# Dot products, key rounds and key products in another order, an inverse's steps cut into quarters, in a fused RWKV-7 and convolution block

## The chip, the cores and the metric

The kernel runs on one core of one Trainium2 chip. The metric is the device time in microseconds of one execution, the median of three runs. TensorE is called PE here, VectorE DVE, ScalarE ACT, GpSimd POOL, and SyncE, which only issues DMAs in this kernel, SP.

## The reference

One layer of a model of width 2048 over 256 tokens, batch 1, in float32. A vector `c` modulates it (shift, scale, gate, twice), then come an RWKV-7 mixer, a feed-forward with a causal convolution of 3 taps and hidden width 5504, and after them a second block. Cut to what matters here:

```python
mod = silu(c) @ ada_w + ada_b            # six vectors of 2048 = 12288 dot products
h = rms(x) * (1 + scale1) + shift1
r, k, v = x_rkv @ w_rkv                  # three 2048x2048 projections
w = decay(w0 + tanh(xw @ w1) @ w2); a = sigmoid(a0 + (xa @ a1) @ a2)
kk = k * k_k; kk = kk * rsqrt(sum(kk*kk, per head))   # "key rounds"
state = state*w + (state a) b + v k      # 256 steps, 32 heads of 64
x = x + gate1 * rms((y * g) @ w_o)
h = rms(x) * (1 + scale2) + shift2
u = conv3(h @ w_in); f = (silu(gate) * val) @ w_out
x = x + gate2 * rms(f)                   # then the second block
```

## The kernel before

Everything lies transposed in SBUF: 16 tiles of 128 channels by 256 tokens. The recurrence is worked in 4 chunks of 64 tokens, with the inverse of a triangular 64x64 matrix for each head and chunk.

**The ring.** Nearly all weights come through `ring`, four slots of 1 MB, which SP fills in a fixed order. The load at position p of that order waits until position p-4 has been used. A load holds one output tile of a projection (`wv`, `wr`, `wo`, `fi`, `fo`) or 128 rows of `ada_w`.

**The dots.** `ada_w` is transposed on the host, so that an output of `mod` is a dot product of one partition's row with `cb` (silu(c) in every partition). One instruction on DVE, line 1683, makes 128 of them from a slot of 1 MB, in place. There are 96: 0 to 31 before the first normalisation, 32 to 37 (two slots of `zb`, loads by POOL, line 565) before the work that prepares keys and decays, 38 to 61 in the ring between tiles of v's projection (two loads of `ada_w` ahead of each load of `wv` from the fifth on), 62 to 79 in the ring during the four chunks of the scan (4, 6, 6, 2), and 80 to 95 in the 16 tiles of the output projection wo, one each, with loads by POOL (line 605). DVE counts them in `ada_used`.

**The keys.** After the dots DVE has a fixed list: elementwise work and prefix sums (1844, 1851), then eight rounds b of the key norm (1869 to 1871), and after rounds 1, 3, 5 and 7 `scaled_keys(q)` (1859 to 1863), which needs rounds 2q and 2q+1 and two exponentials that ACT makes into buffers `px`, `tmp` or `zb` (1354, 1355). The Gram products on PE (844) wait for the fourth `scaled_keys`.

**v and the inverse.** PE projects v in 16 tiles (line 679, 16 matmuls each, evacuated by ACT, 1391). After tiles 8 to 12 it runs one step of the inverse each: two transpositions of the inner inverse (874), one more (884), and two products (893, 902). A step is 64 to 256 small matmuls into four banks of PSUM, and ACT evacuates a bank at a time (1397 to 1410). The scan then alternates between PE (934, 984, 995), DVE (1935 and others) and ACT.

**Split projections.** wo and everything after it works at higher precision: ACT makes `whi` from half a weight slot (1231), DVE subtracts it to get `wlo` (1705), and PE does two matmuls per 128 rows (702, 703), 32 a tile. ACT copies the result out (1238), DVE adds the low part (1713, `join`). For the feed-forward's input `fi` DVE also does two convolution taps per tile (2040, 2041), the first on ACT (1497). `y_lo_part`, line 1974, makes the low part of wo's other operand, and wo's second half waits for the last of them.

**Norms.** The squares of wo's and fo's tiles are summed as the tiles come, by POOL (589, 622); then PE sums over the partitions (661). A third norm, of the sum with the residual (1753, 1755), has its squares on ACT (1200) and is summed on PE (666). The residual is spilled to HBM by a DMA that ACT issues (1475).

PE's order in v, and behind it the line that makes the order of SP's loads there:

```python
for k in range(NT):
    project("v", mixb, k)
    if k == 8:
        pe.wait_ge(base_rdy, 1)
        turned(0)
    elif k == 9:
        turned(1)
```

```python
for _k in range(NT):
    RV += [("v", _k)] + [("ada", len(RV) - NT - _k + _j) for _j in range(0 if _k < 4 else 2)]
```

Of the kernel before, what the change touches and what calls it, by code (L numbers as in the profile page):

```python
# [36 lines left out]
S = 256  # L37
# [22 lines left out]
          ("w2", 1, NT, NT, 0), ("a2", 1, NT, NT, 0), ("r", NT, NT, NT, 0), ("v", NT, NT, NT, 0), ("ada", 42, 0, 0, 0),  # L60
# [24 lines left out]
assert len(RV) == 74 and len(RV_UNIT) == 74  # L85
# [88 lines left out]
def build(nc, t, out, stage=99, dbg=None):  # L174
    with ExitStack() as ctx:
# [87 lines left out]
        ld_ada = [[sem(f"ld_ada{q}_{j}") for j in range(6 - 4 * q)] for q in range(2)]  # L263
# [40 lines left out]
        ld_adw = [sem(f"ld_adw{j}") for j in range(4)]  # L304
        rexp = sem("rexp")
# [114 lines left out]

        MIX = {"r": 0, "k": 1, "v": 2, "w": 3, "a": 4, "g": 5}
        MIX_BUF = {"r": mixa, "v": mixb}
        ADA_PARTS = [(0, 32, 6), (32, 38, 2)]
        ADA_REST = 38
        ada_w = lambda j: ada2[:, j, :] if j < 2 else flat_h[:, 2048 * (j - 2):2048 * (j - 1)]

        def ada_slot(part, j):

            return ada2[:, j, :] if part else ada4[:, j, :] if j < 4 else ada2[:, j - 4, :]
# [127 lines left out]
        def _(pool):  # L557
            def ada(part):
                lo, hi, n = ADA_PARTS[part]

                def load(j, it):

                    src = t["ada"][lo + j] if it is None else \
                        t["ada"][bass.ds(it * n + lo + j, 1)].rearrange("o p n -> (o p) n")
                    pool.dma_start(ada_slot(part, j), src).then_inc(ld_ada[part][j], 16)

                for j in range(n):
                    load(j, None)
                with pool.Fori(1, (hi - lo) // n) as it:
                    for j in range(n):  # L570
                        pool.wait_ge(ada_used, it * n + (lo + j + 1 - n))
                        load(j, it)

            pool.wait_ge(ada_used, 32)
            ada(1)
# [9 lines left out]
            def wo_square(i):  # L585
                pool.wait_ge(tile_free, TILE["wo"] + i + 1)
                if i:
# [7 lines left out]
            for j in range(NT):  # L595
# [7 lines left out]
                if j >= 4:  # L603
                    pool.wait_ge(ada_used, 80 + j - 3)
                pool.dma_start(ada_w(j % 4), t["ada"][80 + j]).then_inc(ld_adw[j % 4], 16)
# [4 lines left out]

            pool.wait_ge(x_spill, 16)
            pool.wait_ge(pe_step, STEP["fo"])
# [37 lines left out]
        def _(pe):  # L651
# [3 lines left out]
            def rms(k, sq, summed=0):  # L655
# [7 lines left out]
                for i in range(NT):  # L663
                    if i % 4 == 0:
                        pe.wait_ge(rms_sq[k], i // 4 + 1)
# [1648 lines left out]
```

## Time and profile before

| | |
|---|---|
| median of 3 runs | 2020.38 us (2018.16 to 2024.25) |
| the profiled execution's own time | 2022.18 us |
| its span, first to last instruction | 2020.5 us |
| granted clock of PE, mean | 0.988 |
| PE busy | 1950.3 us, 97% |
| DVE busy | 1437.4 us, 71% |
| ACT busy | 907.3 us, 45% |
| POOL busy | 107.7 us, 5% |
| moved by DMA | 418.31 MB, mean 207 GB/s |

Busy time is that of instructions; "idle before" names what an engine was released by. A weight load on PE (PEld) overlaps the matmul before it. With PE at 97% the sum of its waits is some 70 us, and what an edit is worth shows in those waits.

### The profile page before, as it was taken

What the parts mean: (1) busy time and instruction counts of PE and PEld (TensorE: products, weight loads), DVE (VectorE), ACT (ScalarE), POOL (GpSimd) and SP (SyncE); (2) the same over time, 40 slices, a digit from 0 to 9 for tenths busy, and PEclk for the clock granted to TensorE, in tenths of its full rate; (3) what the DMA queues carried; (4) which work ended last, traced back from release to release, by engine and by line L of the source; (5) the groups of instructions that cost most, each with busy time, mean ns of one, the idle gap of its engine ahead of it and who ended that gap; (6) DMA issues with size and microseconds to landing.
All of it is one profiled execution on the core that took longest, in us unless ns stands there. A gap on an engine that the chain in (4) does not pass through costs nothing.

```text
span 2020.5 us, 33348 instructions
## 1 busy us (share of the span) xinstructions
PE 1950.3 (97%) x12886; PEld 1688.3 (84%) x12886; DVE 1437.4 (71%) x2023; ACT 907.3 (45%) x1474; POOL 107.7 (5%) x111
## 2 busy tenths in 40 slices
PE   6999899898898989999999999999999999999998
PEld 4888788797887878888888888888878888888887
DVE  7996959535858977777777776444467967766876
ACT  4346221042334545555555555444455436545554
POOL 0000002000002300000000000000010000002200
PEclk9999999899999999999999999999999999999999
DMA  9996414667637925555555556555535544446553
GB/s 393 421 374 213 146 68 162 274 249 298 239 132 285 383 101 187 187 187 187 187 185 186 181 190 230 179 193 193 193 123 213 186 167 175 159 146 222 180 184 124
DMA packets 58933, 418.31 MB, mean 207 GB/s; under 512 B 6673, under 2 KB 7057, under 8 KB 12561
## 3 DMA queue, kind: packets, MB, share of 16 engines
q1 hardware_dynamic: 54514, 383.36, 51.4%
q0 software_dynamic: 3888, 27.26, 3.4%
q10 hardware_dynamic: 432, 6.29, 0.8%
q8 instruction: 70, 1.15, 0.2%
q14 instruction: 29, 0.24, 0.0%
HBM read 410.60 MB, written 6.29 MB: 206 GB/s over the span
## 4 chain that ended last, share of the span: by engine, by line
PE 85%; DVE 8%; DMA 3%; issue 2%; ACT 1%; POOL 1%; SPq 0%; DVEq 0%; POOLq 0%; ACTq 0%
PE ps L702 42%; PE ps L703 21%; PE ps L679 9%; PE ps L803 3%; DVE ring L1683 2%; DMA ring<-in_wv 1%; PE ps L798 1%; DVE ar L1870 1%; DMA bk<-in_ada 1%; PE ps L819 1%; DVE mixb L1921 1%; PE ps L1074 1%; POOL h L601 1%; PE ps L1149 0%; PE ps L768 0%
## 5 line engine op out<-in xcount | busy, mean ns | idle before, releaser
L702 PE MATMUL ps<-x_pair,whi 128*128 128x512 f32 x2464 | 879.1, 401 | 5.3 <-issue 2.8
L703 PE MATMUL ps<-x_pair,wlo 128*128 128x256 f32 x2464 | 692.7, 281 | 0.0
L1705 DVE TENSOR_TENSOR wlo<-ring,whi 128x1024 fp32r<-128x1024 f32 x468 | 547.5, 1206 | 104.7 <-ACT whi L1231 97.2
L702 PEld LDWEIGHTS ps<-x_pair,whi 128*128 128x128 f32 x2464 | 464.3, 188 | 125.1 <-issue 12.0
L1231 ACT ACTIVATE whi<-ring 128x1024 fp32r<-128x1024 f32 x468 | 462.3, 1031 | 96.5 <-PE ps L703 93.8
L703 PEld LDWEIGHTS ps<-x_pair,wlo 128*128 128x128 f32 x2464 | 466.7, 189 | 0.3
L1238 ACT ACTIVATE px<-ps 128x256 f32<-128x256 f32 x202 | 77.8, 385 | 463.3 <-PE ps L703 463.3
L702 PE MATMUL ps<-hid_pair,whi 128*128 128x512 f32 x688 | 238.8, 391 | 0.0
L703 PE MATMUL ps<-hid_pair,wlo 128*128 128x256 f32 x688 | 192.7, 280 | 0.0
L679 PE MATMUL ps<-mixb,ring 128*128 128x256 f32 x640 | 147.5, 393 | 9.0 <-DMA ring<-in_wv 9.0
L702 PEld LDWEIGHTS ps<-hid_pair,whi 128*128 128x128 f32 x688 | 128.7, 187 | 28.5 <-DVE wlo L1705 0.3
L1683 DVE CUSTOM_DVE_ANT_0 ring<-ring,cb,prm 128x2048 f32<-128x2048 f32 x42 | 97.5, 2347 | 74.1 <-DMA ring<-in_ada 73.4
L679 PEld LDWEIGHTS ps<-mixb,ring 128*128 128x128 f32 x640 | 125.8, 198 | 28.7 <-DMA ring<-in_wv 10.2
L703 PEld LDWEIGHTS ps<-hid_pair,wlo 128*128 128x128 f32 x688 | 130.0, 189 | 0.0
L679 PE MATMUL ps<-mixa,ring 128*128 128x256 f32 x512 | 113.2, 384 | 0.0
L679 PEld LDWEIGHTS ps<-mixa,ring 128*128 128x128 f32 x512 | 98.2, 192 | 13.8
L1713 DVE TENSOR_TENSOR px<-ps,px 128x256 f32<-128x256 f32 x134 | 56.4, 421 | 68.4 <-ACT px L1238 68.3
L2040 DVE SCALAR_TENSOR_TENSOR tmp<-px,prm,tmp 128x255 f32<-128x255 f32 x86 | 41.6, 484 | 83.7 <-ACT tmp L1497 83.7
L1768 DVE TENSOR_TENSOR px<-ps,px 128x256 f32<-128x256 f32 x68 | 28.8, 424 | 95.4 <-ACT px L1238 95.1
L702 PE MATMUL ps<-y_pair,whi 128*128 128x512 f32 x256 | 90.4, 397 | 5.2 <-DVE y_pair L1974 3.6
L803 PE MATMUL ps<-mixb,ring 128*128 128x256 f32 x384 | 86.6, 382 | 0.0
L1497 ACT ACTIVATE tmp<-px,prm 128x256 f32<-128x256 f32 x86 | 51.8, 602 | 74.7 <-DVE px L1713 74.7
(297 smaller groups left out, 2308.3 us busy)
## 6 DMA issues: line engine op xcount, KB each, us to landing
ring<-in_fi SPq DMA_DIRECT2D x86, 1024.0 KB, 4.8
ring<-in_zin SPq DMA_DIRECT2D x52, 1024.0 KB, 4.8
ring<-in_ada SPq DMA_DIRECT2D x42, 1024.0 KB, 6.6
ring<-in_fo SPq DMA_DIRECT2D x32, 1024.0 KB, 4.8
bk<-in_ada SPq DMA_DIRECT2D x22, 1024.0 KB, 16.3
ring<-in_wr SPq DMA_DIRECT2D x16, 1024.0 KB, 4.8
ring<-in_wv SPq DMA_DIRECT2D x16, 1024.0 KB, 8.9
ring<-in_wo SPq DMA_DIRECT2D x16, 1024.0 KB, 7.0
```

The costliest lines, as they stand in the source:

```text
L679: last = mm(ps[0:m, bank, 0:S], w[:, k * m:(k + 1) * m], act[:, k, :], start=k == 0, stop=k == n - 1)
L702: mm(ps[:, bank, 0:2 * S], w_h, pair_k, start=first and k == 0, stop=False)
L703: m = mm(ps[:, bank, 0:S], w_l, pair_k[:, 0, :], start=False, stop=last and k == n - 1)
L803: last = mm(outer_bank(m), ring[:, i % RING, m * P:(m + 1) * P], mixb[:, i, :], start=i == 0 and m % 2 == 0, stop=i == NT - 1, skip_group_ ...
L1231: A(whi[:, hf % WB, 0:m], ring[:, u % RING, 1024 * x:1024 * x + m], ACT.Copy).then_inc(w_hi, 1)
L1238: A(part[:, (TILE[name] + k) % 4, :], ps[:, (TILE[name] + k) % BANKS, S:2 * S], ACT.Copy).then_inc(x_part, 1)
L1497: A(tmp[:, (k % 4) * S:(k % 4 + 1) * S], join_in("fi", k, it), ACT.Identity, scale=param_at("fcw", 4 * FT, kk), bias=param_at("fcb", 0, kk ...
L1683: V.tensor_tensor_reduce(out=w, in0=w, in1=cb[:], scale=1.0, scalar=prm[:, m:m + 1], op0=ALU.mult, op1=ALU.add, accum_out=mod[:, m:m + 1]) ...
L1705: V.tensor_tensor(wlo[:, hf % WB, 0:m], ring[:, u % RING, 1024 * x:1024 * x + m], whi[:, hf % WB, 0:m].bitcast(F32), ALU.subtract).then_in ...
L1713: return V.tensor_tensor(o, ps[:, (TILE[name] + k) % BANKS, 0:S], o, ALU.add).then_inc(joined, 1)
L1768: own(V.tensor_tensor(o, ps[:, (TILE[name] + k) % BANKS, 0:S], o, ALU.add))
L2040: own(V.scalar_tensor_tensor(d[:, 1:S], b[:, 0:S - 1], param_at("fcw", 2 * FT, kk), d[:, 1:S], ALU.mult, ALU.add))
```

## The change

It has five parts.

- **A, the dots' places.** 0 to 31 stay. The group ahead of the keys' work has ten (32 to 41), with four slots: two more in `cum`, so ACT's evacuation of w2 into `cum` waits for them. The ring carries 14 during v instead of 24 and 12 during the scan (2, 4, 4, 2) instead of 18. wo still has one a tile (68 to 83). The last twelve (84 to 95) are new in `fi`, one in every second pair of tiles, loads by POOL into the two halves of `mixa`. DVE's first 24 pairs of `fi` are written out instead of looped; the gates' product that needs all 96 dots moves behind them.
- **B, the keys.** `scaled_keys` 0 and 1 come both after round 3, 2 after round 5, 3 after round 7.
- **C, the inverse.** Its five steps move from behind tiles 8 to 12 of v into tiles 9 to 13, each step in quarters, with a quarter after 8, 11, 14 and 16 of the tile's 16 matmuls.
- **D, wo's start.** PE's first two tiles run low half, low half, high half, high half. Their weights' second split comes earlier on ACT and on DVE, there ahead of the last `y_lo_part`.
- **E, the norms.** PE adds the sixteenth square itself instead of POOL. The third norm's last four squares and residuals are in two pieces. The spill is issued by POOL, and DVE waits for it one pair of tiles later.

```diff
-ADA_PARTS = [(0, 32, 6), (32, 38, 2)]
-ADA_REST = 38
+ADA_PARTS = [(0, 32, 6), (32, 42, 4)]
+ADA_REST = 42
+            if part:
+                return ada2[:, j, :] if j < 2 else flat_c[:, 2048 * (j - 2):2048 * (j - 1)]
...
-    RV += [("v", _k)] + [("ada", len(RV) - NT - _k + _j) for _j in range(0 if _k < 4 else 2)]
+    RV += [("v", _k)] + [("ada", len(RV) - NT - _k + _j) for _j in range(0 if _k < 6 else 2 if 8 <= _k < 12 else 1)]
-SCAN_DOTS = (4, 6, 6, 2)
+SCAN_DOTS = (2, 4, 4, 2)
...
+            for k in range(lo, hi):
+                pool.wait_ge(ada_used, max(lo, k + 1 - n))
+                pool.dma_start(ada_slot(1, (k - lo) % n), t["ada"][k]).then_inc(ld_ada[1][(k - lo) % n], 16)
...
+            pool.wait_ge(x_done, NT)
+            pool.dma_start(t["spill"], xr[:].rearrange("p i s -> p (i s)")).then_inc(x_spill, 16)
+            pool.wait_ge(xn_rdy, 4)
             pool.wait_ge(x_spill, 16)
+            for j in range(12):
+                if j >= 2:
+                    pool.wait_ge(ada_used, 84 + j - 1)
+                pool.dma_start(ada_f(j % 2), t["ada"][84 + j]).then_inc(ld_adf[j % 2], 16)
...
 +            for k in range(INV_TILE, INV_TILE + 5):
+                u = RV_UNIT["v", k]
+                unit_in(u)
+                bank_free(TILE["v"] + k)
+                for b, (lo, hi) in enumerate(((0, 8), (8, 11), (11, 14), (14, 16))):
+                    for x in range(lo, hi):
+                        m = mm(ps[:, (TILE["v"] + k) % BANKS, 0:S], ring[:, u % RING, x * P:(x + 1) * P], mixb[:, x, :],
+                               start=x == 0, stop=x == NT - 1)
+                    if b == 3:
+                        m.then_inc(pe_step, 1)
+                    inverse(k - INV_TILE, b)
...
 -            project_split("wo", tiles_of(y_pair), NT, x_rdy=((y_lo, 2), (y_lo, 4)))
+            two_by_halves("wo", tiles_of(y_pair), ((y_lo, 2), (y_lo, 4)))
+            project_split("wo", tiles_of(y_pair), NT, first=2)
             keep_clock(5, 6)
-            rms(1, None, NT)
+            rms(1, None, NT - 1, (TILE["wo"] + NT, mixb[:, NT - 1, :]))
...
 +            act.wait_ge(ada_used, 40)
             evac("w2", NT, lambda i, b: A(at_tile(cum, i), b, ACT.Sigmoid, bias=param_at("w0", 0, i)))
...
 -                if b % 2:
+                for q in {3: (0, 1), 5: (2,), 7: (3,)}.get(b, ()):
                     dve.wait_ge(hs_used, b + 1)
-                    scaled_keys(b // 2)
+                    scaled_keys(q)
...
                      join("fi", k, it)
+                    if e == 0 and dot is not None:
+                        dve.wait_ge(ld_adf[dot % 2], 16 * (dot // 2 + 1))
+                        dot_into(84 + dot, ada_f(dot % 2))
                     dve.wait_ge(cv_act, k + 1 if it is None else it * 4 + (k + 1))
...
-            for it in own.loop((FT - 3) // 2, 8):
+            for j in range(1, 24):
+                conv_pair(j, None, 2 * j, j // 2 if j % 2 else None)
```

In PE's order, v's projection and the first steps of the inverse; `ring` holds v's weights, `mixb` the input, `zb` and `cst` the inner inverse and the identity. Before:

```order
L679 MATMUL ps<-mixb,ring 128x256 x144
L874 MATMUL ps<-cst,zb 64x64 x64
L679 MATMUL ps<-mixb,ring 128x256 x16
L874 MATMUL ps<-cst,zb 64x64 x64
L679 MATMUL ps<-mixb,ring 128x256 x16
L884 MATMUL ps<-cst,zb 64x64 x64
L679 MATMUL ps<-mixb,ring 128x256 x16
L893 MATMUL ps<-cum,h 64x32 x128
```

and now:

```order
L689 MATMUL ps<-mixb,ring 128x256 x144
L953 MATMUL ps<-mixb,ring 128x256 x8
L898 MATMUL ps<-cst,zb 64x64 x16
L953 MATMUL ps<-mixb,ring 128x256 x3
L898 MATMUL ps<-cst,zb 64x64 x16
L953 MATMUL ps<-mixb,ring 128x256 x3
L898 MATMUL ps<-cst,zb 64x64 x16
L953 MATMUL ps<-mixb,ring 128x256 x2
```

The first 144 matmuls (nine tiles) are as they were. Then each 64-matmul step, which stood whole between two tiles, stands in four runs of 16 inside one tile, a tile later.

In SP's order, the loads for v's tiles: `in_wv` is a tile of v's weights, `in_ada` a load for a dot. Before, to the end of v's first seven tiles:

```order
L471 DMA ring<-in_wv 128x2048 x5
L471 DMA ring<-in_ada 128x2048 x2
L471 DMA ring<-in_wv 128x2048
L471 DMA ring<-in_ada 128x2048 x2
L471 DMA ring<-in_wv 128x2048
```

and now, to the end of the first eleven:

```order
L477 DMA ring<-in_wv 128x2048 x7
L477 DMA ring<-in_ada 128x2048
L477 DMA ring<-in_wv 128x2048
L477 DMA ring<-in_ada 128x2048
L477 DMA ring<-in_wv 128x2048
L477 DMA ring<-in_ada 128x2048 x2
L477 DMA ring<-in_wv 128x2048
L477 DMA ring<-in_ada 128x2048 x2
L477 DMA ring<-in_wv 128x2048
```

Each tile of v has two more megabytes loaded beside it from the fifth on before, and none, one or two now.

In DVE's order, the first tile of an odd pair in `fi` (the pair's second tile follows it): the half splits of the weights (`wlo`), the gated product of the pair before (`tmp`, `hid_pair`), the join (`px<-ps,px`), and the taps. Now:

```order
L1759 TENSOR_TENSOR wlo<-ring,whi 128x1024 x2
L2080 TENSOR_TENSOR tmp<-tmp 128x256
L2082 CAST hid_pair<-tmp 128x256
L2083 TENSOR_TENSOR hid_pair<-tmp,hid_pair 128x256
L1767 TENSOR_TENSOR px<-ps,px 128x256
L1737 ISA mixa,mod<-mixa,cb,prm 128x2048
L1737 ISA mod 128x1
L2103 SCALAR_TENSOR_TENSOR tmp<-px,prm,tmp 128x255
L2104 SCALAR_TENSOR_TENSOR tmp<-px,prm,tmp 128x254
L1759 TENSOR_TENSOR wlo<-ring,whi 128x1024 x2
```

The two rows of 1737, the dot and the reading of its sum, stand between the join and the first tap, and the next tile's two splits behind the taps. Everything else in these rows stood there before, in a loop, with register instructions between.

## Rows read from the trace of the kernel before

A float32 matmul stands as two records in PE's rows of plain projections and of the inverse, so a tile of v is x32 there.

**Rows 1.** PE's waits: what line waited for, us in total, times, longest.

```profile
PE ps L679 <- DMA ring<-in_wv: 9.0, 3, 3.1
PE ps L844 <- DVE bk L1863: 7.1, 1, 7.1
PE ps L995 <- DVE cum L1935: 4.7, 3, 2.3
PE ps L702 <- DVE y_pair L1974: 3.6, 1, 3.6
PE ps L661 <- POOL sq_sum L589: 0.8, 1, 0.8
```

**Rows 2.** Timeline around the keys: start, us, instruction, idle before and releaser.

```profile
202.84 1.23 DVE L1859 TENSOR_TENSOR bk<-bk,mixb 128x1024 f32<-128x1024 f32 x1 [2.54 <-ACT tmp L1355]
```

**Rows 3.** Timeline of the dots ahead of the keys.

```profile
168.87 2.35 DVE L1683 CUSTOM_DVE_ANT_0 zb<-zb,cb,prm 128x2048 f32<-128x2048 f32 x1 [3.47 <-DMA zb<-in_ada]
174.23 2.35 DVE L1683 CUSTOM_DVE_ANT_0 zb<-zb,cb,prm 128x2048 f32<-128x2048 f32 x1 [3.00 <-DMA zb<-in_ada]
```

**Rows 4.** Window ahead of them: us, busy PE, PEld, DVE, ACT, POOL; PEclk, DMA share, GB/s.

```profile
145.00:150.00 5.00, 5.00 (x25) 4.41 (x24) 4.93 (x8) 5.00 (x18) 0.38 (x1) 1.00 0.34 138
```

**Rows 5.** Timeline of v's tiles and the inverse.

```profile
363.18 0.38 ACT L1391 ACTIVATE mixa<-ps 128x256 f32<-128x256 f32 x1 [6.52 <-PE ps L679]
373.18 15.77 PE L679 MATMUL ps<-mixb,ring 128*128 128x256 f32 x64 [3.13 <-DMA ring<-in_wv]
391.87 10.23 PE L679 MATMUL ps<-mixb,ring 128*128 128x256 f32 x32 [2.93 <-DMA ring<-in_wv]
405.91 7.17 PE L679 MATMUL ps<-mixb,ring 128*128 128x256 f32 x32
423.99 7.31 PE L884 MATMUL ps<-cst,zb 64*64 64x64 f32 x128
426.02 8.48 ACT L1404 ACTIVATE cum<-ps 32x512 f32<-32x512 f32 x8 [1.53 <-PE ps L884]
461.44 0.58 PE L902 MATMUL ps<-h,cum 64*32 64x32 f32 x14 [4.37 <-issue]
461.95 16.23 PE L679 MATMUL ps<-mixb,ring 128*128 128x256 f32 x64
```

**Rows 6.** Windows there.

```profile
392.00:394.00 2.00, 2.00 (x5) 1.64 (x6) 0.00 (x0) 0.00 (x0) 0.00 (x0) 0.50 0.99 414
460.00:462.00 2.00, 0.56 (x15) 0.49 (x14) 0.33 (x3) 0.00 (x0) 0.00 (x0) 0.50 1.03 430
462.00:464.00 2.00, 2.00 (x6) 1.64 (x6) 2.00 (x1) 1.18 (x2) 0.00 (x0) 0.50 0.13 49
```

**Rows 7.** Timeline of two chunks of the scan.

```profile
530.70 3.30 PE L995 MATMUL ps<-cum,zb 128*64 128x64 f32 x64 [1.90 <-DVE cum L1935]
552.72 2.34 DVE L1683 CUSTOM_DVE_ANT_0 ring<-ring,cb,prm 128x2048 f32<-128x2048 f32 x1
556.25 2.09 PE L995 MATMUL ps<-cum,zb 128*64 128x64 f32 x64 [2.31 <-DVE cum L1935]
```

**Rows 8.** Timeline from wo to the third norm.

```profile
649.78 2.83 DVE L1683 CUSTOM_DVE_ANT_0 h<-h,cb,prm 128x2048 f32<-128x2048 f32 x1
734.30 1.06 ACT L1200 ACTIVATE mixb<-mixa 128x1024 f32<-128x1024 f32 x1 [1.41 <-DVE mixa L1755]
```

**Rows 9.** Timeline of two tiles in `fi`.

```profile
1220.69 0.39 ACT L1238 ACTIVATE px<-ps 128x256 f32<-128x256 f32 x1 [1.82 <-PE ps L703]
1221.32 0.42 DVE L1713 TENSOR_TENSOR px<-ps,px 128x256 f32<-128x256 f32 x1
1222.47 0.48 DVE L2040 SCALAR_TENSOR_TENSOR tmp<-px,prm,tmp 128x255 f32<-128x255 f32 x1 [0.73 <-ACT tmp L1497]
1223.42 2.36 DVE L1705 TENSOR_TENSOR wlo<-ring,whi 128x1024 fp32r<-128x1024 f32 x2
1226.34 0.39 ACT L1238 ACTIVATE px<-ps 128x256 f32<-128x256 f32 x1 [2.00 <-PE ps L703]
```

More of the change, by code:

```diff
@@ L304, in build @@
         ld_adw = [sem(f"ld_adw{j}") for j in range(4)]
+        ld_adf = [sem(f"ld_adf{j}") for j in range(2)]
         rexp = sem("rexp")
@@ L557, in _ @@
         def _(pool):
[L558 to L575, printed above, removed]
+            lo, hi, n = ADA_PARTS[1]
+            for k in range(lo, hi):
+                pool.wait_ge(ada_used, max(lo, k + 1 - n))
+                pool.dma_start(ada_slot(1, (k - lo) % n), t["ada"][k]).then_inc(ld_ada[1][(k - lo) % n], 16)
             pool.sem_inc(ar_rdy, 1)
@@ L720, in one @@
                             first_half()
+                for k in range(first, 4 if first else 0):
+                    one(k, None)
                 looped = n // 4 * 4 if n >= 8 and not between else 0
                 if looped:
-                    with pe.Fori(0, n // 4) as it:
+                    with pe.Fori(1 if first else 0, n // 4) as it:
                         for k in range(4):
@@ L865, in _ @@
             HC = CH // 2
-            def turned(half):
-                for b in range(4):
-                    if half:
-                        pe.wait_ge(e_tt, b + 1)
-                    for t in range(32 * half + 8 * b, 32 * half + 8 * b + 8):
-                        for o in (0, CH):
-                            m = mm(ps[o:o + CH, 4 + b, t % 8 * CH:(t % 8 + 1) * CH], pair[o:o + CH, t, :],
-                                   ident[o:o + CH, o:o + CH], start=True, stop=True)
-                    m.then_inc(c_tt, 1)
@@ L898, in t2_a21_t1, with turned @@
-            def t2_a21_t1():
-                pe.wait_ge(e_tt, 16)
-                for n in range(2 * CH // 2):
+            def turned(half, b):
+                if half:
+                    pe.wait_ge(e_tt, b + 1)
+                for t in range(32 * half + 8 * b, 32 * half + 8 * b + 8):
+                    for o in (0, CH):
+                        m = mm(ps[o:o + CH, 4 + b, t % 8 * CH:(t % 8 + 1) * CH], pair[o:o + CH, t, :],
+                               ident[o:o + CH, o:o + CH], start=True, stop=True)
+                m.then_inc(c_tt, 1)
@@ new lines, in _ @@
+            for k in range(INV_TILE):
+                project("v", mixb, k)
+            for k in range(INV_TILE, INV_TILE + 5):
+                u = RV_UNIT["v", k]
[8 more added lines that the diff above has]
+                    inverse(k - INV_TILE, b)
@@ L921, in _ @@
+            for k in range(INV_TILE + 5, NT):
+                project("v", mixb, k)
             pe.wait_ge(ar_rdy, 5)
```

222 lines of the change are left out of this document (132 added, 90 removed).

## The prediction

> **What bounds the kernel now.** I read the page first: PE is busy for 1950.3 of 2020.5 us, so an edit pays only where it ends a wait of PE or one of its stretches at half clock. PE's waits by releaser come second [rows 1]. The change touches the waits of v's tiles for their weights (9.0 us), of the Gram products for the last keys (7.1), of the scan for a DVE copy (4.7), of wo for the low part of its operand (3.6) and of the norm for POOL's last sum (0.8). The timeline of these places comes third; there the reader is to see what DVE or the DMA queues did when PE stood still. The clock column of the windows is last: behind one of v's waits, and in its last inverse step, the granted clock is 0.50, that is 1.2 of 2.4 GHz [rows 6], so a wait costs more than its length.
>
> **B, the keys.** DVE idles 2.54 us ahead of the first `scaled_keys`, since ACT's exponential isn't there [rows 2]. Rounds 2 and 3 now stand in that place; from their end DVE has the same work left and never lacks an exponential, since the next ones have `px` free only one key product later and have two more rounds to be made in. The fourth product ends 2.5 us sooner, and PE's wait of 7.1 [rows 1] falls to 4.6: **-2.5**.
>
> **A, ahead of the keys.** Four more dots of about 2.3 us and four more loads of 1 MB stand before DVE's list, which PE waits for later, so each microsecond of delay here is one of the total. Today DVE does not do the dots back to back: the last start 5.36 us apart (168.87, 174.23) and wait 3.47 and 3.00 us for their loads [rows 3], since two slots allow two loads at a time. With four slots, four loads are out from the start, when the two first ones were before, and each later one leaves four dots ahead, not two. Between 145 and 150 us the DMA engines are busy 0.34 of the time [rows 4]: there is room for the extra ones. If the tenth dot's load leaves when the fourth's last did before, it lands in the same time, and the tenth ends where the sixth did, near 176.5: **0**. The lower bound is -1, by one gap that closes earlier. The upper bound is two more gaps of 5.36, +10.7: the queue then gives only the old rate for the two dots which no early load covers. I take 0, nearer the free queue of 145 to 150. ACT's new wait ahead of w2's evacuation ends with the eighth dot, one gap and one dot (5.36 + 2.3) before the tenth, near 169. Behind it in ACT's queue are the evacuations of w2 and a2, from which the keys' factors come, and PE's banks hang on them. I cost it at nothing: a few us late there still lie within the 4.6 that PE waits for the keys.
>
> **A and C, v's tiles.** A tile of v takes 6.52 + 0.38 = 6.9 us by ACT's copies, which follow it, 6.91 over many [rows 5]. Three waits for `wv`: two [rows 5] of 3.13 and 2.93 and a third like them sum to 9.0 [rows 1]. A load of `wv` leaves behind two of `ada_w`, and the queues are full then, at 414 GB/s [rows 6]: 3 MB take 7.6 us, more than a tile. Now tiles up to the seventh have none ahead, and those with two ahead have the inverse's quarters in them, 7.31 us a step [rows 5]: **-9.0**. After two of the waits PE ran at half clock: 64 records took 15.77 where two tiles need 13.82 at full clock, and one tile took 10.23 where one between two steps takes 7.17 [rows 5]: 1.95 + 3.06, **-5.0**. Near the end of the last step PE stood 4.37 us for nothing that the profile shows, "issue", and the two tiles after it took 16.23, begun at 0.50 clock [rows 6], for some 14.1 (7.17 + 6.91) [rows 5]. With 3 to 8 projection matmuls between quarters and fewer loads beside them I expect no such stop: **-4.4 - 2.1 = -6.5**. Step 3 now waits for all of step 2's evacuations. ACT needs 8.48/4 = 2.12 us for a quarter of it [rows 5]; the next tile's first eight matmuls give it 6.91/2 = 3.45, so I expect no stop, and 2.1 at most. What the quarters do cost is turns between the two kinds of matmul. The tile between two steps takes 7.17 and not 6.91, 0.26 for one turn in and out; 15 turns more at that price are 3.9. Part of the 0.26 is the end of the last matmul, which runs beside what follows, so I take **+1.0**, between 0 and 3.9. I add 0.3 for the first tile with two dots beside it, tile 9: its load leaves behind two others, with no quarters before it. Together **-19.2**.
>
> Of the stop called issue, the rows say this: it ended between 460 and 462, where the DMA share was 1.03 and 430 GB/s, and in the next window the share is 0.13 [rows 6]. So it ends with the loads. That speaks for a fetch of instructions that has to queue behind weights, and the change then removes it. The Trainium skill ("Runtime: NRT & Kernel Launch", section "Instruction fetch mechanics") says that the sequencer fetches blocks of 256 instructions by its own DMA queue, and that the crossing is mostly hidden. By that sentence the stop isn't a fetch, has another cause, and may stay; this is rival 1, and the sum would be 6.5 higher.
>
> **The scan.** DVE does a ring dot of 2.34 us right before the copy that PE waits for (552.72, PE released at 556.25 after 2.31); in another chunk the wait is 1.90 and the stretch after it takes 3.30 instead of 2.09 [rows 7]. With two dots fewer per chunk the copy comes up to 4.7 us sooner. All 4.7 of waits [rows 1] go, and 1.2 of slow clock with them, less 0.5 since a dot may still lie in the way in one chunk: **-5.4**. Lower bound 0, if the remaining dots stand in the same places ahead of the copies.
>
> **D, wo.** The 3.6 us of wait [rows 1] at wo's second half could be covered with the second tile's low half (half a tile of 5.65 [rows 9]). But the DVE is then the pace: per tile it has two splits (2.36) and a join (0.42) [rows 9] and a dot (2.83 beside POOL's adds [rows 8]), 5.6 in all. What PE gains at the start it waits for a few tiles later: **0**, between -3 and +0.6.
>
> **E, the norms.** POOL's sixteenth add is off the path: -0.8 at wo [rows 1], and the same at fo, taken at the same size. The last quarter of the squares (1.06 us, after a wait of 1.41 for the residual [rows 8]) is halved, and so is the residual: 0.5 + 0.6 = 1.1. Sum **-2.6**. The spill is costed at nothing: DVE waits for it today at the start of fi, but PE waits nowhere in [rows 1] for what DVE makes then, and the first splits, made before, cover it. With no such cover it would be the write of 2 MB at the 414 GB/s of [rows 6], 5 us, once.
>
> **A, fi.** Twelve dots come between join and taps. By the timeline [rows 9], with ACT's copy at 1220.69 as zero: join ends at +1.05, the dot at +3.32 (2.27 from start to start), the taps (0.95) at +4.27, the first half of the split at +5.45. PE begins the tile that needs it about when ACT copies the one before, 1226.34 - 1220.69 = +5.65, less the 0.2 that I estimate between a tile's last matmul and ACT's start: +5.45. So the dot just fits in a tile of 5.65; for the signal between engines I charge 0.15: **+1.8**. DVE's slack (0.56 us from the second split's end to 1226.34, and the 0.73 ahead of the taps, in each tile [rows 9]) absorbs the rest before the next dot, four tiles on. Bounds: 0 and 0.7 each (+8.4), if the looped pairs of today, whose taps come later, are the right measure. What is queued behind the dot's wait for its load is the taps, the next `wlo`, and so PE. A slot's load has two dots' distance, eight tiles of 5.65, so it isn't late.
>
> **Sum.** -2.5 + 0 - 19.2 - 5.4 + 0 - 2.6 + 1.8 = -27.9 against the profiled execution's own 2022.18 us: 1994.3. That execution is 1.8 over the median, and by the median it is 1992.5. I say **1994** for the likeliest case.
>
> **Rivals.**
> 1. *The issue stop stays.* It waits for nothing the trace names, and its cause may be the long run of small matmuls, which the quarters keep. Against it: it ends as the loads do. It gives back 6.5: 2000.5. Chance 0.24.
> 2. *The ten dots end late.* The queues are open in [rows 4] alone for sure; where they are full, two more loads out slow the others. For it: waits of 3 us at each of today's dots [rows 3]. Ends +10.7: about 2005. Chance 0.09.
> 3. *A dot in fi costs 0.7.* +8.4 in place of 1.8: 2000. Chance 0.07.
> 4. *The ring's waits stay* (the change doesn't do what the loads' order says). Each two-load tile still lacks its weights, and 9.0 + 5.0 stay: 2008. Against it: the quarters give such a tile over 7 us more. Chance 0.07.
> 5. *Slower.* The dot in fi isn't covered at all: DVE is the pace of a pair, or POOL's loads land behind SP's, and each dot pushes PE by its own length, 2.83 at the longest [rows 8], or more with its load's wait. The gain of 29.7 elsewhere is used up from 2.5 per dot on; 12 x 2.83 = 34 gives 2026. For over 0.3% slower a dot must cost 3.0. For it: DVE has only 1.3 us of slack in such a tile [rows 9]. Against it: the count above. Chance 0.03.
> The likeliest case has 0.50.
>
> **The numbers.** The likeliest's own range is 1988 to 1999, from D at -3 and the scan or fi at their bounds. Rivals 1 to 3 lie at 2000 to 2005, so 1988 to 2005 leaves out rival 4 and rival 5 and some of 2. A measurement of this kernel tells about 0.3% (6.1 us) from no change, so faster is below 2014.3: 0.93; same 0.04, slower 0.03.
>
> **What would show it.** In the profile after: no wait of v's matmuls for `in_wv` and no window at 0.50 clock there; no wait of over 2 us on ACT before the inverse's first product; no issue stop of 4 us in the steps (rival 1 otherwise); PE's wait for `bk` near 4.6, above 7 if rival 2 holds; the last of the ten dots ending near 176.5; waits of the scan for the copy under 0.5; in fi, PE's waits for `wlo` summing to 2 (8 for rival 3, 30 for rival 5). The forecast is wrong if the tiles with quarters run at half clock, because PE now stops briefly four times as often.

## The result and the profile after

The changed kernel takes 2006.26 us, the median of 20 runs (1996.56 to 2013.01), against 2017.84 us for the kernel before, also of 20 (2007.16 to 2027.19). The ratio is 0.9943, 95% interval 0.9927 to 0.996: 11.6 us faster. The forecast was 28 us and 1994, its range ended at 2005. The profiled execution of the change has a span of 2004.9 us against 2020.5. So the two profiles differ by 15.6 us, 4 us more than the medians, since the first profile of the kernel before was one of its slower executions (2022.18 against 2017.84).

PE's waits after, those that answer to [rows 1] and the new ones:

```profile
PE ps L844 <- ACT cum L1380: 5.1, 1, 5.1
...
PE ps L869 <- DVE bk L1922: 3.4, 1, 3.4
...
PE ps L712 <- DVE wlo L1759: 2.6, 1, 2.6
...
PE ps L953 <- DMA ring<-in_wv: 0.7, 1, 0.7
PE ps L1035 <- DVE cum L1995: 0.6, 3, 0.2
```

The waits for v's weights (9.0) are down to 0.7, those of the scan for DVE's copy (4.7) to 0.6, the wait for the keys (7.1) to 3.4, the stop called issue in the inverse is gone (one of 2.4 us in the scan is there), and wo's 3.6 has become 2.6. New is the first line: PE waits 5.1 us for ACT to evacuate w2 into `cum`. The timeline there, ahead of the keys:

```profile
168.82 0.53 POOL L567 DMA_DIRECT2D zb<-in_ada  x1 [5.42 <-DVE mod L1737]
...
173.83 2.35 DVE L1737 CUSTOM_DVE_ANT_0 cum<-cum,cb,prm 128x2048 f32<-128x2048 f32 x1 [1.38 <-DMA cum<-in_ada]
...
176.53 1.57 ACT L1380 ACTIVATE cum<-ps,prm 128x256 f32 x4 [5.55 <-DVE mod L1737]
177.05 15.08 PE L844 MATMUL ps<-tmp,ring 96*128 96x256 f32 x56 [5.14 <-ACT cum L1380]
178.18 2.35 DVE L1737 CUSTOM_DVE_ANT_0 zb<-zb,cb,prm 128x2048 f32<-128x2048 f32 x1 [1.99 <-DMA zb<-in_ada]
...
181.25 2.35 DVE L1737 CUSTOM_DVE_ANT_0 zb<-zb,cb,prm 128x2048 f32<-128x2048 f32 x1 [0.71 <-DMA zb<-in_ada]
```

The eighth dot starts at 173.83, ACT's new wait ends with it at 176.5, and PE with ACT at 177.05. The tenth dot starts at 181.25, where the sixth of before started at 174.23 [rows 3]. The windows show what was behind it (us, busy times, then PE's clock, DMA share and GB/s):

```profile
170.00:175.00 5.00, 1.92 (x9) 1.33 (x7) 3.53 (x3) 0.75 (x2) 0.00 (x0) 1.00 1.02 423
175.00:180.00 5.00, 2.95 (x7) 2.41 (x8) 3.01 (x3) 2.52 (x6) 0.00 (x0) 0.56 0.83 346
```

The queues are full (share 1.02, 423 GB/s) until the last loads are in, and PE, having stood, goes on at a mean clock of 0.56. One quartered step of the inverse, with the matmuls of v's tile on line 953, reads:

```profile
409.16 3.72 PE L953 MATMUL ps<-mixb,ring 128*128 128x256 f32 x16
412.81 1.15 PE L898 MATMUL ps<-cst,zb 64*64 64x64 f32 x32
413.88 1.56 PE L953 MATMUL ps<-mixb,ring 128*128 128x256 f32 x6
...
420.09 1.15 PE L898 MATMUL ps<-cst,zb 64*64 64x64 f32 x32
421.17 3.72 PE L953 MATMUL ps<-mixb,ring 128*128 128x256 f32 x16
```

A quarter of this step is 32 records. From 409.16 to 421.17 are 12.01 us; whole, the tile took 6.91 + 0.26 and the step 3.95 less what they overlap, 10.98 from start to start in the kernel before. The quarters cost 1.0 us a step.

The stages, by the starts of their first matmuls on PE, in us (forecast is the prediction's term for the stage):

```
stage                              before   after   difference   forecast
w2's first matmul to head sums      13.9    21.9      +8.0         0
head sums to Gram products          69.4    65.7      -3.7        -2.5
Gram products to v                  75.2    76.5      +1.3         0
v, with the inverse                160.4   144.8     -15.6       -19.2
scan and gate, to wo               135.0   130.0      -5.0        -5.4
wo, to the sum of squares           97.4    95.7      -1.7        -0.8
norms, to fi                        26.1    25.7      -0.4        -1.1
fi                                 490.1   490.1       0          +1.8
the rest                           783.1   784.4      +1.3        -0.7
```

The first two rows belong together. DVE's list of key work starts when its last dot ends, and the Gram products start when the list ends:

```
                                last dot ends   Gram products start   between
before                             176.59            253.25            76.66
experiment 5 (B alone)             176.76            250.82            74.06
changed kernel                     183.60            257.65            74.05
changed kernel, second profile     183.12            257.18            74.06
experiment 1 (six dots)            175.48            249.53            74.05
experiment 2                       188.99            263.04            74.05
```

With part B the list takes 74.05 us in each version, whether ACT waits ahead of w2 (the changed kernel) or not (experiments 1, 2 and 5). So the changed kernel's Gram products start 4.4 us later than before because the last dot ends 7.0 later and the list is 2.6 shorter, and for no other reason.

### The profile page after: what moved, and what is told of

It reads as the page before. It is cut to its first block, busy times and chain, and to the rows that moved or that the text cites. A ratio compares the mean times of both kernels' runs of the same rounds, so it can differ in the third digit from the quotient of the medians.

```text
span 2004.9 us, 32849 instructions
## 1 busy us (share of the span) xinstructions
PE 1954.1 (97%) x12890; PEld 1686.4 (84%) x12890; DVE 1436.5 (72%) x2025; ACT 909.5 (45%) x1475; POOL 121.2 (6%) x126
## 4 chain that ended last, share of the span: by engine, by line
PE 87%; DVE 6%; DMA 4%; issue 2%; POOL 1%; ACT 1%; SPq 0%; ACTq 0%; DVEq 0%; POOLq 0%
PE ps L712 43%; PE ps L713 22%; PE ps L689 6%; PE ps L828 3%; PE ps L953 2%; DMA cum<-in_ada 2%; DVE ar L1929 1%; PE ps L823 1%; DMA bk<-in_ada 1%; PE ps L985 1%; PE ps L1115 1%; PE ps L844 1%; PE ps L974 1%; POOL h L596 1%; PE ps L1024 0%
## 5 line engine op out<-in xcount | busy, mean ns | idle before, releaser
L712 PE MATMUL ps<-hid_pair,whi 128*128 128x512 f32 x688 | 243.3, 399 | 0.0
L1737 DVE CUSTOM_DVE_ANT_0 ring<-ring,cb,prm 128x2048 f32<-128x2048 f32 x26 | 60.5, 2349 | 77.4 <-DMA ring<-in_ada 77.2
L689 PE MATMUL ps<-mixb,ring 128*128 128x256 f32 x480 | 104.2, 379 | 0.0
L689 PEld LDWEIGHTS ps<-mixb,ring 128*128 128x128 f32 x480 | 91.1, 190 | 12.4
L828 PE MATMUL ps<-mixb,ring 128*128 128x256 f32 x384 | 86.3, 382 | 0.0
L828 PEld LDWEIGHTS ps<-mixb,ring 128*128 128x128 f32 x384 | 73.7, 192 | 10.3
```

The lines of the kernel that those rows point to most:

```text
L689: last = mm(ps[0:m, bank, 0:S], w[:, k * m:(k + 1) * m], act[:, k, :], start=k == 0, stop=k == n - 1)
L712: mm(ps[:, bank, 0:2 * S], w_h, pair_k, start=first and k == 0, stop=False)
L828: last = mm(outer_bank(m), ring[:, i % RING, m * P:(m + 1) * P], mixb[:, i, :], start=i == 0 and m % 2 == 0, stop=i == NT - 1, skip_group_ ...
L1737: V.tensor_tensor_reduce(out=w, in0=w, in1=cb[:], scale=1.0, scalar=prm[:, m:m + 1], op0=ALU.mult, op1=ALU.add, accum_out=mod[:, m:m + 1]) ...
```

## The experiments

All ratios are to the kernel before, run again beside each set of experiments (medians 2014.69 to 2018.65). The executions of one kernel spread by some 20 us, so where a stage of the trace tells the cases apart, it decides. The diffs are cut to the lines that matter.

**1. Six dots ahead of the keys, sixteen in fi.** From the changed kernel:

```diff
-        ADA_PARTS = [(0, 32, 6), (32, 42, 4)]
+        ADA_PARTS = [(0, 32, 6), (32, 38, 2)]
...
-            act.wait_ge(ada_used, 40)
...
-                conv_pair(j, None, 2 * j, j // 2 if j % 2 else None)
+                conv_pair(j, None, 2 * j, j - 1 - j // 3 if j % 3 else None)
```

> The changed kernel with six dots ahead of the keys again (two slots, no wait of ACT ahead of w2) and sixteen instead of twelve in fi, in two pairs of three. Theory A, the four extra dots and their loads are what cost time ahead of the keys: PE's wait of 5.1 us ahead of w2's matmuls and the half clock behind it are gone, the head sums start near 184 us instead of 192, the Gram products near 251 instead of 258, the median about 7 us under the changed kernel's, ratio to the kernel before near 0.991. Rival, the early half clock in the changed kernel is chance and the time comes back as a longer wait for the keys: Gram products still near 257, ratio near 0.994. If a dot in fi costs 0.7 us, 3 us of the gain are lost again.

Ratio 0.9909 (0.9876 to 0.9942), median 1993.22, span 1989.5. The last dot on DVE, and PE at w2 and at the Gram products:

```profile
169.85 14.05 PE L844 MATMUL ps<-tmp,ring 96*128 96x256 f32 x64
173.13 2.35 DVE L1736 CUSTOM_DVE_ANT_0 zb<-zb,cb,prm 128x2048 f32<-128x2048 f32 x1 [3.99 <-DMA zb<-in_ada]
...
249.53 1.69 PE L869 MATMUL ps<-ar,bk 64*64 64x64 f32 x36 [3.47 <-DVE bk L1921]
```

w2's 64 records take 14.05 us again without a wait, and the Gram products start at 249.53 instead of 257.65. The last dot ends 8.1 us sooner than in the changed kernel, and the Gram products start 8.1 us sooner. A part of that is chance: with six dots the last one ended between 175.4 and 176.8 in eight profiles, with ten in the change's slots between 183.1 and 183.6 in four, so the four extra dots cost 7.5 us of path on the mean. Theory A stands; the rival, that the time comes back as a longer wait for the keys, falls (3.47 against 3.35).

**2. The slots in `cum` used once.**

```diff
-                pool.wait_ge(ada_used, max(lo, k + 1 - n))
-                pool.dma_start(ada_slot(1, (k - lo) % n), t["ada"][k]).then_inc(ld_ada[1][(k - lo) % n], 16)
+                s = j if j < 4 else j % 2
+                pool.wait_ge(ada_used, lo if j < 4 else lo + j - 3 if j < 6 else lo + j - 1)
+                pool.dma_start(ada_slot(1, s), t["ada"][k]).then_inc(ld_ada[1][s], 16)
...
-            act.wait_ge(ada_used, 40)
+            act.wait_ge(ada_used, 36)
```

> The changed kernel, but the two slots in cum are used once (dots 34 and 35); dots 36 to 41 go through the two slots of zb, and ACT waits for 36 dots instead of 40. It still does ten dots ahead of the keys. If ACT's wait for cum is what costs (theory A1), PE's wait of 5.1 ahead of w2 is gone and the Gram products start near 251 to 253. If the lateness of the dots on DVE is what costs (theory A2), the wait ahead of w2 is gone and PE waits for the keys instead, longer than the 3.4 us of the changed kernel, by 5 to 9 us, so the Gram products start at 257 or later and the ratio is 0.994 or more.

Ratio 0.9967 (0.994 to 0.9994). PE's waits:

```profile
PE ps L871 <- DVE bk L1925: 8.9, 1, 8.9
PE ps L856 <- DVE ar L1906: 5.9, 1, 5.9
```

And DVE's last dot:

```profile
186.63 2.35 DVE L1739 CUSTOM_DVE_ANT_0 zb<-zb,cb,prm 128x2048 f32<-128x2048 f32 x1 [3.60 <-DMA zb<-in_ada]
```

The wait at w2 is gone, and the time is not: the head sums wait 5.9 us for what DVE makes behind its dots, the Gram products 8.9, and these start at 263.0. This version has fewer slots, and its last dot ends 5.4 us later than the change's, so the start at 263.0 alone would not decide between A1 and A2. What decides is the distance from the last dot's end to the Gram products: 74.05 us, as in the changed kernel, where ACT's wait is there. So A2 stands: it is the lateness of the dots on DVE, and ACT's wait only moves PE's idle time to an earlier place.

**3. The inverse's steps whole.**

```diff
+            for k in range(NT):
+                project("v", mixb, k)
+                if 8 <= k <= 12:
+                    for b in range(4):
+                        inverse(k - 8, b)
```

> The changed kernel with the inverse's five steps whole, behind tiles 8 to 12 of v, as in the kernel before. Theory as in the prediction, the fewer dots in the ring end the waits for v's weights and the stop called issue: from v's start to the scan's start no more than 2 us over the changed kernel's 144.8. Rival, the quarters do it, by giving time between loads and by breaking up the small matmuls: the waits for v's weights come back at tiles 9 to 11 (3 us each) or the issue stop does (4 us), and the stage takes 5 to 12 us more.

Ratio 0.9919 (0.9893 to 0.9944), no slower than the change; v takes 144.4 us against 144.8. The waits for v's weights are gone without the quarters. (ACT's order of evacuations follows PE's, as before.) But one part of the theory fell: the stop called issue is there again, in the fifth step.

```profile
446.10 4.04 PE L921 MATMUL ps<-h,cum 64*32 64x32 f32 x242
453.74 0.41 PE L921 MATMUL ps<-h,cum 64*32 64x32 f32 x14 [3.59 <-issue]
```

What the DMA queues did from 450.6 to 452.6, in the middle of the stop, and from 452.6 to 454.2, at its end:

```profile
q1 hardware_dynamic: 104, 0.83, 99.4%
q8 instruction: 1, 0.02, 2.8%
```

```profile
q1 hardware_dynamic: 30, 0.11, 17.5%
```

The queue of instructions moves one packet while PE stands. In the second window the weights' queue is at 17.5% and PE still stands until 453.74, so the end of the loads isn't what releases it. The packet is. In the four profiles with a whole fifth step in which PE stops there, by the times of the packets (us):

```
                                PE stops   packet starts   packet ends   PE goes on   between the last two
before                           457.07       459.08          460.06       461.44          1.38
before, second profile           452.09       453.98          454.96       456.35          1.39
experiment 5                     449.61       450.68          451.65       453.03          1.38
experiment 3                     450.14       451.43          452.34       453.74          1.40
```

Each packet is one of 16 KB. Whether it starts so late because it queues behind the weights is not shown: the weights' queue was full ahead of it in all four. Fewer loads did not end the stop; the quarters did (its line isn't among PE's waits of the change, above 0.5). They win 3.6 us and the slow clock behind it and pay 1.0 five times: nothing is left.

**4. No dots in fi.** The twelve dots and their loads are left out, the second gate takes other columns.

```diff
-            for j in range(12):
-                if j >= 2:
-                    pool.wait_ge(ada_used, 84 + j - 1)
-                pool.dma_start(ada_f(j % 2), t["ada"][84 + j]).then_inc(ld_adf[j % 2], 16)
...
-                conv_pair(j, None, 2 * j, j // 2 if j % 2 else None)
+                conv_pair(j, None, 2 * j, None)
```

> The changed kernel without the twelve dots in fi and their loads (left out: the last 1536 outputs of the modulation; the second gate takes the columns of the second scale). As predicted, a dot in fi costs 0.15 us: 1.8 us less, hardly to be measured (ratio to the changed kernel 0.999). Rival, 0.7 us each: 8 us less. The stage fi in the trace tells it: its length from the first to the last matmul.

Ratio 0.9925 (0.99 to 0.995), median 2001.58; fi takes 479.5 us instead of 490.1. By itself that is 0.9 us a dot, beyond the rival. But the tiles tell something else: here every tile of fi takes 5.55 us, those far behind the last dot's place too, and in the change each takes 5.65, with dot or without. ACT's copies of two tiles here:

```profile
905.12 0.38 ACT L1275 ACTIVATE px<-ps 128x256 f32<-128x256 f32 x1 [1.72 <-PE ps L709]
910.67 0.38 ACT L1275 ACTIVATE px<-ps 128x256 f32<-128x256 f32 x1 [1.93 <-PE ps L709]
```

86 tiles at 0.1 us are 8.6 of the 10.6 us. Another 1.7 come from 3.4 us at half clock at the start of the changed kernel's fi, which this profile lacks. That leaves next to nothing for the dots' own tiles.

**5. The order of the keys alone**, on the kernel before.

```diff
-                if b % 2:
-                    dve.wait_ge(hs_used, b + 1)
-                    scaled_keys(b // 2)
+                for q in {3: (0, 1), 5: (2,), 7: (3,)}.get(b, ()):
+                    dve.wait_ge(hs_used, b + 1)
+                    scaled_keys(q)
```

> The kernel before with part B alone, the order of the keys' products. As predicted: the idle 2.5 us of DVE ahead of the first product is filled, the Gram products start 2.5 us earlier (250.7 instead of 253.3), PE's wait for the keys is 4.6 instead of 7.1, nothing else moves. Rival, the first exponentials or the free buffers come later than thought and DVE idles behind a later round: 0.

```profile
PE ps L844 <- DVE bk L1863: 4.7, 1, 4.7
```

4.7 us of wait for 7.1, and the Gram products start at 250.82 instead of 253.25: 2.4 us, as forecast. In the whole it can't be measured: 0.9994 (0.997 to 1.0018).

**6. The quarters alone**, on the kernel before: the functions of the change for the inverse, and its order on PE and ACT.

```diff
+            for k in range(INV_TILE, INV_TILE + 5):
...
+                    inverse(k - INV_TILE, b)
```

> The kernel before with part C alone, the inverse's steps in quarters inside tiles 9 to 13 of v. Theory now: the quarters end the stop called issue (4.4 us and 2.1 of slow clock), because an instruction fetch takes longer than a run of small matmuls lasts, and cost about 1 us a step (5.1 in all), so with the waits for v's weights unchanged (9.0, or fewer where the quarters give the loads time) v takes 155 to 160 us instead of 160.4. Rival, the prediction's: the quarters cost 1.0 in all and v takes 154 or less; and if the ring's dots are what makes the stop, it is still there.

Ratio 1.0006 (0.9981 to 1.0032); v takes 156.5 us, which is what it takes in the second profile of the kernel before too (156.3, experiment 8), so the quarters alone win nothing: what the stop gave back went into the turns. The waits for v's weights are still 10.0 in all:

```profile
PE ps L680 <- DMA ring<-in_wv: 7.8, 3, 3.2
...
PE ps L929 <- DMA ring<-in_wv: 2.2, 1, 2.2
```

So it is the number of dots in the ring that ends these waits, and the quarters end only the stop. A part of the forecast for a rival is wrong with it: the quarters don't give the loads enough time by themselves.

**7. Six dots ahead, one step in quarters.** From experiment 1, the first four steps whole behind tiles 8 to 11, the fifth in quarters in tile 12.

```diff
+            for k in range(12):
+                project("v", mixb, k)
+                if k >= 8:
+                    for b in range(4):
+                        inverse(k - 8, b)
+            for k in range(12, 13):
```

> The version with six dots ahead of the keys and sixteen in fi, with only the fifth step of the inverse in quarters (in tile 12 of v) and the first four whole behind tiles 8 to 11. Theory: each quartered step costs about 1 us of turns between kinds of matmul, and the stop of 3.6 us comes only in the fifth step, so v takes 4 us less than with all in quarters: 140 to 141 us instead of 144.6. Rival, the stop moves into the fourth step or behind it: 143 to 145.

Ratio 0.9898 (0.988 to 0.9915). v takes 139.9 us, 4.7 less than with all in quarters (144.6 in experiment 1), and the fifth step has no stop:

```profile
428.73 3.72 PE L956 MATMUL ps<-mixb,ring 128*128 128x256 f32 x16
432.38 1.20 PE L921 MATMUL ps<-h,cum 64*32 64x32 f32 x64
...
439.82 1.20 PE L921 MATMUL ps<-h,cum 64*32 64x32 f32 x64
440.95 20.99 PE L689 MATMUL ps<-mixb,ring 128*128 128x256 f32 x96
```

**8. The kernel before, once more**, unchanged.

> The kernel before, unchanged, for a second profile. In the first, a tile of fi took 5.65 us, in the changed kernel without its dots 5.55, without a change in what PE does. If the pace is a property of the code (the loop, or the dots), it is 5.65 again in all of fi; if it is a state that an execution falls into, tiles of 5.55 can be there, and fi takes up to 8 us less (482 instead of 490).

Span 2008.5 us, 12 less than in the first profile of the same kernel. Its fi takes 480.2 us, with tiles of 5.55 from the second on. First ACT's copies, then a window of 20 us of the first profile and of this one:

```profile
904.40 0.39 ACT L1238 ACTIVATE px<-ps 128x256 f32<-128x256 f32 x1 [1.71 <-PE ps L703]
909.95 0.39 ACT L1238 ACTIVATE px<-ps 128x256 f32<-128x256 f32 x1 [1.51 <-PE ps L703]
```

```profile
900.00:920.00 20.00, 20.00 (x115) 17.37 (x114) 15.27 (x25) 11.24 (x17) 0.00 (x0) 1.00 0.55 206
```

```profile
900.00:920.00 20.00, 20.00 (x117) 17.66 (x116) 14.83 (x24) 11.68 (x17) 0.00 (x0) 1.00 0.59 210
```

**9. The changed kernel, once more**, unchanged.

> The changed kernel, unchanged, for a second profile. Its head sums start at 192 and its Gram products near 257.6 again, whatever the clock does, since the late dots are its own. The pace of fi's tiles may be 5.55 for a while and turn to 5.65 at a dot, as with sixteen dots, or be 5.65 from the start, as in its first profile.

Span 1989.8 us. The late dots are there again: head sums at 191.3, Gram products at 257.2. fi begins at 5.55 and turns at a dot:

```profile
765.12 0.39 ACT L1279 ACTIVATE px<-ps 128x256 f32<-128x256 f32 x1 [1.72 <-PE ps L713]
770.66 0.39 ACT L1279 ACTIVATE px<-ps 128x256 f32<-128x256 f32 x1 [1.92 <-PE ps L713]
776.33 0.39 ACT L1279 ACTIVATE px<-ps 128x256 f32<-128x256 f32 x1 [1.55 <-PE ps L713]
```

The dot stands on DVE from 765.92 to 768.3, and holds up the half split for the next tile of PE. That tile, which ends at 776.33, took 5.67, and all others up to fi's end 5.65. fi took 487.8.

**10. fi's dots in the second tile of a pair**, from experiment 7.

```diff
-                    if e == 0 and dot is not None:
+                    if e == 1 and dot is not None:
```

> The version with six dots ahead of the keys and one step in quarters, with fi's dots in the second tile of a pair instead of the first. There DVE has no gated product, the join ends 0.2 us sooner, and the half split that PE waits for is ready 0.2 us before it is needed. Theory: a dot in the first tile delays PE by 0.1 to 0.3 us, and one such delay turns the pace of all later tiles from 5.55 to 5.65 us; so now the tiles stay at 5.55, fi takes 478 to 481 us instead of 487.6, and the median is up to 7 us lower. Rival, the pace changes by chance: tiles of 5.65 again, fi 485 or more.

Ratio 0.9883 (0.9854 to 0.9911), median 1990.39, fi 485.9 us. The theory fell: fi began at 5.65, tiles with a dot took up to 5.98, and the pace turned both ways at dots; behind the last of them it stayed at 5.55. So the second tile is no better covered than the first, and a dot can end the slow pace as well as begin it.

**11. wo's old start**, from experiment 7.

```diff
-            two_by_halves("wo", tiles_of(y_pair), ((y_lo, 2), (y_lo, 4)))
-            project_split("wo", tiles_of(y_pair), NT, first=2)
+            project_split("wo", tiles_of(y_pair), NT, x_rdy=((y_lo, 2), (y_lo, 4)))
...
```

> The version with six dots ahead of the keys and one step in quarters, without part D: wo's first two tiles whole, the second tile's splits where they were. As predicted, D is worth nothing over all of wo, since DVE sets the pace there: wo to the sum of squares 95 to 97 us as before. Rival, D's gain of 1.1 us at the first tiles (wait of 2.5 instead of 3.6) stays: 1 us more than with D.

Ratio 0.9885 (0.9854 to 0.9916), not to be told from experiment 7. wo took 97.8 us to the sum of squares against 95.8, with the wait for `y_pair` at 3.7 again instead of 2.5 for `wlo`. 1.2 of the 2.0 us are this wait; this profile also has 6.8 us at half clock in wo, against 3.4, with tiles of 5.55 in both. The two profiles of the kernel before, also with 3.4 us at half clock and tiles of 5.55, take 97.4 and 97.6, of which 0.8 is the wait for POOL that E ends. So D is worth 0.8 to 1.0, and the rival's 1 us stands: DVE, though busy nearly all the time, did not take the gain back.

## Why the prediction was wrong

**The step that failed** is "A, ahead of the keys", with its value of 0: "If the tenth dot's load leaves when the fourth's last did before, it lands in the same time, and the tenth ends where the sixth did, near 176.5". The last load left at 168.82 and its dot began at 181.25; before, the sixth's left at 166.05 and its dot began at 174.23. The tenth dot ended at 183.6 (183.1 in the second profile) instead of 176.5. I had taken one window with a DMA share of 0.34 [rows 4] for room. On both sides of the room the queues were full or nearly so. The windows, one of before and two of after:

```profile
140.00:145.00 5.00, 5.00 (x25) 4.41 (x24) 4.79 (x13) 2.49 (x8) 0.00 (x0) 1.00 0.84 318
```

```profile
140.00:145.00 5.00, 5.00 (x25) 4.38 (x24) 4.79 (x13) 2.40 (x8) 0.00 (x0) 1.00 1.01 421
145.00:150.00 5.00, 5.00 (x25) 4.41 (x24) 4.93 (x8) 5.00 (x17) 0.53 (x1) 1.00 0.98 406
```

Between 140 and 150 us the queues moved 1.9 MB more than before; that was the room, under half of the four loads' 4.2 MB. A sum by bytes, as an estimate from these rows, would have told: 4.2 MB at the 414 GB/s of [rows 6] take 10.1 us, less 4.5 for 1.9 MB of room, so some 6 us late and not 0; 7.0 were measured. That today's dots already waited 3 us for each load [rows 3] was the sign that the loads were the pace. The prediction's own sentence on the price held to 0.1 us: "each microsecond of delay here is one of the total". The last dot came 7.0 us later and the Gram products 4.4, which is 7.0 less the 2.6 of B. Experiments 1 and 2 show it.

**ACT's new wait** had been costed at nothing, "a few us late there still lie within the 4.6 that PE waits for the keys", and cost nothing in the end, though PE stood 5.1 us for it and lost 2.9 more at the slow clock behind it (8.0 in the stage). DVE's list ran its 74.05 us regardless, and PE would have stood for it anyway: with B alone it waits 4.7 for the keys, and with dots 6.8 us later it would wait 11.5. In the changed kernel 5.1 + 2.9 + 3.4 = 11.4. That is also why PE's wait for `bk` did not rise above 7, the sign named for rival 2: its idle time lay elsewhere.

**Rival 2**, with a chance of 0.09, has the right cause: the ten dots end late. It priced them at 10.7, and 7.0 were measured. That its time of 2005 lies near 2006.26 is in part luck, since the quarters and the base were wrong as well.

**v.** Forecast -19.2, measured -15.6. The ring's waits came out as reckoned (9.0 to 0.7), and the stop went. The cost of the quarters was mis-sized: 1.0 in the sum, 5.1 in the trace (1.0 each), beyond even the upper bound of 3.9, because that bound took the turns of a whole step as all there is between two kinds of matmul. The reason given for the stop's end was a misreading: "so it ends with the loads". In the kernel before PE goes on at 461.44, while the loads run until 462.7; in experiment 3 it goes on behind the bulk of them; in both it is 1.4 us behind the packet of instructions. That it is a fetch fits these times. That fewer loads would end it was wrong, and that it queues behind weights is open. The stop went by the quarters alone (experiments 3 and 6).

**Keys, scan, norms.** B was right to 0.1 us (2.4 of 2.5 in experiment 5, and 2.6 by the length of DVE's list). The scan gave 5.0 of 5.4, though the stage spreads by some 6 us between profiles (127 to 133 with the changed order). D was put at 0 and is worth about 1 us (experiment 11). E was put at 2.6 (its terms add up to 2.7). At wo it gave its 0.8, in the norms 0.4 of 1.1; at fo the spread of the rest hides it.

**fi.** 1.8 was forecast and the two first profiles differ by 0, but that is no proof: both ran at the slow pace. Between profiles that began at the fast pace the dots cost some 8 us (487.8 with twelve dots, 479.5 without, 480.2 in the kernel before), nearly all by turning the pace and not by delaying their own tiles. The sum's 0.15 per dot for the signal between engines stands in no row; where a trace shows such a signal, from the end of DVE's last key product to PE's start, it is 0.06. Whether an execution is in the slow pace at fi's start is not explained; so the mean cost of the dots lies between 0 and 8, and the ratios of experiment 4 and of the change (0.9925 and 0.9943) say some 3.6, with intervals that overlap.

**The base.** The sum was made against one execution of 2022.18 us, at the slow pace in fi and with much half clock in v. It promised back 7.1 us of slow clock in v, of which the second profile of the kernel before lacks some 4 already. Against the median of 20, 2017.84, the same sum of -27.9 would have ended at 1990, 16 us under what was measured. As an estimate, 7.0 for the late dots, 4.1 for the quarters and 4.1 for the base in v are 15 of these 16.

The version of experiment 7 beats both kernels, 0.9898 (0.988 to 0.9915) against the change's 0.9943 (0.9927 to 0.996). Experiments 1 (0.9909), 10 (0.9883) and 11 (0.9885) can't be told from it.

## What to carry to other kernels

Where an engine already waits for each load, the loads are the pace: price the added megabytes at the rate of the full queue, and take off the free time of the queue counted in megabytes too, before it is called room. Work put ahead of an engine's fixed list delays the end of the list by its full lateness; the time that another engine waits there is that engine's slack and not the list's. Cutting a stop out by interleaving has its own price per turn, so cut only the piece that has the stop.

## What the runs showed of the hardware

- The same matmuls on PE, with no wait and a granted clock of 1.00, run at two paces: 5.55 or 5.65 us for a tile of 16 pairs of matmuls. The slow one is a rhythm of three pairs, 349, 350 and 361 ns apart, where the fast one of the same kernel has 346 or 347. A pace lasts for hundreds of us, in the kernel before through all 86 tiles of fi, and turns at a small disturbance, in both directions (experiments 4, 8, 9, 10). It is no matter of fi alone: wo ran at 5.55 in the first profile of the kernel before, whose fi ran at 5.65, and wo at 5.65 in experiment 2, whose fi began at 5.55. Over fi that is 8.6 us, a good part of the spread of 20 us between runs of one kernel. What sets it stays open.
- PE stopped for 3.4 to 4.4 us after 242 records of small matmuls, in every version in which the fifth step was whole, and in none where it was in quarters. It went on 1.38 to 1.40 us after the end of a 16 KB packet on the instruction queue. Over all thirteen profiles there are 19 stops of PE called issue of over 1 us up to the end of the scan, and each ends 1.2 to 1.5 us after the end of such a packet. (A stop of 2.8 us far behind the scan, in each profile, is of another kind: the last such packet lies 16 us or more back.) All this fits an instruction fetch that PE waits for; it is read from the times of the packets and not shown by an experiment on the fetch itself. Why the packet starts only 1.1 to 2.0 us after PE has stopped in the fifth step stays open. The Trainium skill ("Runtime: NRT & Kernel Launch", section "Instruction fetch mechanics") says that such a crossing is mostly hidden. These traces don't agree for runs of short matmuls: the records stand 16 ns apart (4.04 us for 242), and the crossing cost 3.4 to 4.4 us. In the nine profiles with the fifth step in quarters no stop showed there.
